# A two-layer decoder trunk on one core: memory normalised at evacuation, announced branches, the last expert pair by halves, the final norm applied at evacuation

## The reference

```python
def reference(...):
    mem_n = rms_norm(mem, norm_mem)
    for i in range(DEPTH):
        h = rms_norm(x, norm_mix[i])
        ...
            x = x + conformer_conv(h, ...)      # layer 0
        ...
            x = x + gla_mixer(h, ...)           # layer 1
        x = x + mem_cross_attn(rms_norm(x, norm_xattn[i]), mem_n, xa_w_q[i], xa_w_kv[i], xa_w_o[i])
        x = x + hier_moe(rms_norm(x, norm_ffn[i]), ...)
    return rms_norm(x, norm_final)

def rms_norm(x, g):
    y = xf * lax.rsqrt(jnp.mean(xf * xf, axis=-1, keepdims=True) + EPS)
    return (y * g.astype(jnp.float32)).astype(x.dtype)
```

## Time and profile before

| | us |
|---|---|
| median of three runs | 1923.87 |
| runs | 1920.25, 1923.87, 1925.53 |
| profiled execution | 1920.17 |
| its span in the profile | 1918.0 |
| PE busy | 1864.5 |
| DVE busy | 583.6 |
| ACT busy | 373.6 |
| POOL busy | 159.9 |

### The profile page before, as it was taken

One profiled execution on the slowest core, in us unless ns is written; L12 is line 12 of the kernel. 1 busy time (PEld: TensorE's weight loads), 2 busy tenths in 40 slices (PEclk: granted clock), 3 DMA queues, 4 the chain that ended last, 5 costly groups with the idle time before them and its releaser, 6 DMA issues.

```text
span 1918.0 us, 18457 instructions
## 1 busy us (share of the span) xinstructions
PE 1864.5 (97%) x7584; PEld 924.7 (48%) x7584; DVE 583.6 (30%) x1104; ACT 373.6 (19%) x629; POOL 159.9 (8%) x151
## 2 busy tenths in 40 slices
PE   6999999998999999999999999999989999999997
PEld 5445644545445454444344444454454444445443
DVE  3899221223122222222212322213222222222223
ACT  2333211212111011111124232122111111111113
POOL 0466210010000000000020000100100000000001
PEclk9999999998999999999999999999989999999998
DMA  9214422102999999999861211302169999999992
GB/s 352 74 46 169 174 88 88 74 17 105 414 404 406 412 403 416 405 412 406 336 224 44 88 44 44 132 1 91 44 260 415 404 413 407 413 406 403 415 411 88
DMA packets 89869, 477.08 MB, mean 249 GB/s; under 512 B 7662, under 2 KB 8092, under 8 KB 40236
## 3 DMA queue, kind: packets, MB, share of 16 engines
q1 hardware_dynamic: 88636, 470.90, 61.2%
q0 software_dynamic: 592, 2.63, 0.5%
q10 hardware_dynamic: 544, 2.22, 0.3%
HBM read 471.53 MB, written 4.19 MB: 248 GB/s over the span
## 4 chain that ended last, share of the span: by engine, by line
PE 90%; DVE 7%; ACT 1%; issue 1%; DMA 0%; SPq 0%; DVEq 0%; ACTq 0%
PE PS L617 23%; PE PS L435 17%; PE PS L391 13%; PE PS L632 12%; PE PS L655 7%; PE PS L672 7%; DVE PS L1752 5%; PE PS L920 3%; PE PS L530 2%; PE PS L442 1%; PE PS L662 1%; PE PS L644 1%; PE PS L681 1%; DVE PS L1750 1%; PE PS L875 0%
## 5 line engine op out<-in xcount | busy, mean ns | idle before, releaser
L435 PE MATMUL PS<-hT,ring 128*128 128x512 f32 x640 | 279.4, 596 | 4.1 <-ACT hT L1149 3.4
L632 PE MATMUL PS<-ring,hT 128*64 128x512 f32 x1024 | 226.8, 595 | 2.7 <-ACT hT L1250 2.7
L617 PE MATMUL PS<-ring,hT 128*64 128x512 f32 x1024 | 226.3, 595 | 1.3 <-DVE small L1631 1.3
L617 PE MATMUL PS<-ring,xg 128*64 128x512 f32 x1024 | 226.8, 595 | 0.0
L1640 DVE TENSOR_TENSOR xT<-PS,xT 128x512 f32<-128x512 f32 x256 | 158.5, 681 | 211.6 <-PE PS L655 211.6
L435 PEld LDWEIGHTS PS<-hT,ring 128*128 128x128 f32 x640 | 121.4, 191 | 153.3 <-issue 152.4
L617 PEld LDWEIGHTS PS<-ring,hT 128*64 128x64 f32 x1024 | 73.9, 137 | 132.9 <-issue 131.2
L617 PEld LDWEIGHTS PS<-ring,xg 128*64 128x64 f32 x1024 | 72.4, 137 | 132.4 <-issue 132.2
L632 PEld LDWEIGHTS PS<-ring,hT 128*64 128x64 f32 x1024 | 70.7, 137 | 135.1 <-issue 127.9
L1666 DVE TENSOR_TENSOR ylo<-PS,yhi 128x1024 fp32r<-128x1024 f32 x32 | 39.2, 1224 | 301.7 <-ACT yhi L1255 301.7
L655 PE MATMUL PS<-onehotT,yhi 128*128 128x512 f32 x256 | 115.0, 449 | 3.6 <-DVE ylo L1666 3.6
(11 more groups left out here) (263 smaller groups left out, 1768.8 us busy)
## 6 DMA issues: line engine op xcount, KB each, us to landing
ring<-in_moe_w_gate SPq DMA_DIRECT2D x128, 1024.0 KB, 11.2
ring<-in_moe_w_up SPq DMA_DIRECT2D x128, 1024.0 KB, 12.1
ring<-in_moe_w_down SPq DMA_DIRECT2D x128, 1024.0 KB, 9.0
ring<-in_xa_w_kv SPq DMA_DIRECT2D x16, 1024.0 KB, 7.3
ring<-in_gla_w_in SPq DMA_DIRECT2D x12, 1024.0 KB, 12.8
ring<-in_conv_w_in SPq DMA_DIRECT2D x8, 1024.0 KB, 14.2
ring<-in_xa_w_q SPq DMA_DIRECT2D x8, 1024.0 KB, 6.8
ring<-in_xa_w_o SPq DMA_DIRECT2D x8, 1024.0 KB, 6.9
```

The source lines that it names most:

```text
L435: mm = pe.matmul(bank(b), w[:, k * 512 + m * P:k * 512 + (m + 1) * P], src[:, k, :], start=(k == 0), stop=(k == C - 1))
L617: mm = pe.matmul(PS[e * SL:(e + 1) * SL, kind * BANK:(kind + 1) * BANK], x[:, k, (2 * (p % 2) + e) * SL:(2 * (p % 2) + e + 1) * SL], ring[ ...
L632: mm = pe.matmul(PS[e * SL:(e + 1) * SL, (2 + half) * BANK:(3 + half) * BANK], hidT[:, k, e * SL:(e + 1) * SL], ring[:, pair_slot(l, 4 + e ...
```

## The change

It has four parts. The memory is transposed as it was loaded, in two transfers with a semaphore each; its reciprocal norms are spread over the partitions by two products with diagonals (key `rbm`) and multiplied in, with the gain, when the transposes are evacuated; `mem_k(0, 0)` waits chunk by chunk. The three small loads ahead of the memory go to ACT's queue. In both layers the last pair's down projection is computed by output halves, with the transposed one-hot between them, and `yhi`, `ylo` and the scatter follow by halves. The branch over the overflow code is written out on PE, ACT and DVE and announced by a hint, placed behind pair 13 on PE and behind pair 8 on ACT and DVE; in layer 1 PE's waits for the last accumulates are moved behind the sums. At the end PE transposes `xT` itself; the gain `norm_final` is loaded as a row, broadcast to all partitions by a transfer of POOL's, and multiplied in at DVE's evacuations, or by POOL behind ACT's for the three blocks in `GAINED`; ACT loads its table first and only squares; POOL adds five squares and DVE the other three; the output is stored in eight half tiles.

```diff
 HOTS = NQ + TT - 1
...
 
...
         osum = small[:, 12:28]
...
                     for m in (2 * jj, 2 * jj + 1):
-                        mm = group(bank(b, (m % 2) * NMEM, (m % 2 + 1) * NMEM),
-                                   lambda k: w[:, k * 512 + m * P:k * 512 + (m + 1) * P],
-                                   lambda k: memT[:, k, :], C)
+                        for k in range(C):
+                            if l == 0 and i == 0 and m == 0:
+                                pe.wait_ge(mem_chunk, k + 1)
+                            mm = pe.matmul(bank(b, (m % 2) * NMEM, (m % 2 + 1) * NMEM),
+                                           w[:, k * 512 + m * P:k * 512 + (m + 1) * P], memT[:, k, :],
...
 
+                def down_half(p, half):
+                    pe.wait_ge(g["hidT_ready"], NP * r + p + 1)
+                    for k in range(FC):
+                        if k % 2 == 0:
+                            for e in range(2):
+                                loaded(p, 4 + e, k // 2)
+                        for e in range(2):
+                            mm = pe.matmul(PS[e * SL:(e + 1) * SL, (2 + half) * BANK:(3 + half) * BANK],
+                                           hidT[:, k, e * SL:(e + 1) * SL],
+                                           ring[:, pair_slot(l, 4 + e), k * D + half * 512:k * D + (half + 1) * 512],
+                                           start=(k == 0), stop=(k == FC - 1))
+                    mm.then_inc(g["y_full"], 1)
...
                         b, done = use(p, 1 + c)
                         for w in (yhi, ylo):
                             mm = pe.matmul(bank(b), w[:, c * P:(c + 1) * P], onehotT[:, :],
...
-                    down(p)
-                    if more:
-                        gather(q + 1, p, 10, 4 * s + 2)
-                    one_hot_T(p)
+                    if p < NP - 1:
+                        down(p)
+                        if more:
+                            gather(q + 1, p, 10, 4 * s + 2)
+                        one_hot_T(p)
+                    else:
+                        down_half(p, 0)
+                        one_hot_T(p)
+                        down_half(p, 1)
...
+                    if main and p == NP - 3:
+                        ahead = pe.mark_branch_hint_location()
...
-            pe.wait_ge(mem_ready, 2)
             for j in range(4):
-                transposes(("mt", j), [mem_tm[:, mt, c * P:(c + 1) * P] for c in (2 * j, 2 * j + 1) for mt in range(2)])
-            for j in range(4):
-                pe.wait_ge(*read(("mt", j)))
+                take(("mt", j))
+            for mt in range(2):
+                pe.wait_ge(s_mld[mt], 16)
+                for c in range(C):
+                    b = plan.at[("mt", c // 2)][0]
+                    mm = pe.transpose(bank(b, c % 2 * NMEM + mt * P, c % 2 * NMEM + (mt + 1) * P),
+                                      mem_tm[:, mt, c * P:(c + 1) * P], ident[:, :])
+                    if mt and c % 2:
+                        mm.then_inc(bank_full[b], 1)
+            b = take(("rbm",))
+            for mt in range(2):
+                pe.wait_ge(mem_ready, mt + 1)
+                mm = pe.matmul(bank(b, mt * P, (mt + 1) * P), ones[:, :], dg[:, mt, :], start=True, stop=True)
+            mm.then_inc(bank_full[b], 1)
             mem_k(0, 0)
...
-                worst = moe_segment(l, 0)
-                with pe.If(worst > SL):
+                worst, ahead = moe_segment(l, 0)
...
+                nc.switch_bb(f"pe_on{l}")
+                if l == 0:
+                    for b in range(3):
+                        pe.wait_ge(seg[l][f"x_read{b}"], PER_ROUND)
 
             moe(0)
...
-            for c in range(C):
-                wait_h(pe, LAST, c)
+            def turn_out(c, t):
+                if c % 4 == 0:
+                    take(("out", t, c // 4), (0, 1, 2, 3, 5, 6, 7, 4)[t + c])
+                b = plan.at[("out", t, c // 4)][0]
+                mm = pe.transpose(bank(b, c % 4 * P, (c % 4 + 1) * P), xT[:, c, t * P:(t + 1) * P], ident[:, :])
+                if c % 4 == 3:
+                    mm.then_inc(bank_full[b], 1)
+
+            for c in range(4):
+                wait_x(pe, LAST, c)
+                for t in range(TT):
+                    turn_out(c, t)
+            pe.wait_ge(norm_sum, LAST - 1)
+            token_sums(("rs", LAST), [dg[:, :, :].rearrange("p t s -> p (t s)")], 4)
+            for b in range(3):
+                pe.wait_ge(seg[1][f"x_read{b}"], PER_ROUND)
             for t in range(TT):
-                for half in range(2):
-                    if (t, half) == (2, 0):
-                        norm_sums(LAST)
-                    transposes(("out", t, half), [hT[:, 4 * half + j, t * P:(t + 1) * P] for j in range(4)])
...
-            vector_rows(sp, list(VROWS)[:NFIRST], s_vfirst)
-            sp.dma_start(mem_tm[:, :, :], a["mem"].rearrange("b (t p) d -> p (b t) d", p=P)).then_inc(s_mld, 16)
+            for i in range(2):
+                sp.dma_start(mem_tm[:, i, :], a["mem"].rearrange("b (t p) d -> p (b t) d", p=P)[:, i, :]
+                             ).then_inc(s_mld[i], 16)
...
-            for t in range(TT):
-                for half in range(2):
-                    sp.wait_ge(*read(("out", t, half)))
-                sp.dma_start(o_dram[t], x_tm[:, t, :]).then_inc(s_out, 16)
-            sp.wait_ge(s_out, 16 * TT)
+            for half in range(2):
+                cols = slice(half * 512, (half + 1) * 512)
+                for t in range(TT):
+                    if (t, half) in GAINED:
+                        sp.wait_ge(out_gained, GAINED.index((t, half)) + 1)
+                    else:
+                        sp.wait_ge(*read(("out", t, half)))
+                    sp.dma_start(o_dram[t][:, cols], x_tm[:, t, cols]).then_inc(s_out, 16)
...
-            norm_adds(LAST)
+            pool.dma_start(gain_row, a["norm_final"].rearrange("(o d) -> o d", o=1).to_broadcast([P, D])).then_inc(s_gain, 16)
+            for c in range(1, 5):
+                pool.wait_ge(sq_ready, C * (LAST - 2) + c + 1)
+                if c > 1:
+                    pool.wait_ge(early_adds, c - 1)
+                pool.tensor_tensor(rms, hT[:, c, :], hT[:, 0, :] if c == 1 else rms, ALU.add).then_inc(early_adds, 1)
+            pool.wait_ge(s_gain, 16)
+            for n, (t, half) in enumerate(GAINED):
+                cols = slice(half * 512, (half + 1) * 512)
+                pool.wait_ge(out_scaled, n + 1)
+                pool.tensor_tensor(x_tm[:, t, cols], x_tm[:, t, cols], gain_row[:, cols], ALU.mult).then_inc(out_gained, 1)
...
+                    else:
+                        act.activation(yhi[:, 0:512], bank(2), ACT.Copy).then_inc(g["yhi_done"], 1)
...
+                    if p == NP - 1:
+                        act.wait_ge(g["y_full"], YS * r + NP + 1)
+                        act.activation(yhi[:, 512:1024], bank(3), ACT.Copy).then_inc(g["yhi_done"], 1)
...
                               w[j * WDW_ROWS:(j + 1) * WDW_ROWS, :]).then_inc(s_wdw, 16)
             act.wait_ge(s_constp, NCONST)
...
-            act.wait_ge(s_mld, 16)
             ebf = EB[:, :, :].rearrange("p a t -> p (a t)")
             for mt in range(2):
+                act.wait_ge(s_mld[mt], 16)
                 link(act.activation(ebf, mem_tm[:, mt, :], ACT.Square, accum_out=mstat[:, mt:mt + 1]))
...
+            act.activation(small[:, 150:151], ones[:, 0:1], ACT.Sqrt)
             for c in range(C):
-                square(LAST, c)
-                gain(LAST, c)
+                wait_x(act, LAST, c)
+                act.activation(hT[:, c, :], xT[:, c, :], ACT.Square).then_inc(sq_ready, 1)
             norm_root(LAST)
             act.wait_ge(rb_ready, 2)
-            for t in range(TT):
-                evacuate(("out", t, 1), x_tm[:, t, 512:1024], scale=rrec[:, t:t + 1])
+            for t, half in GAINED:
+                evacuate(("out", t, half), x_tm[:, t, half * 512:(half + 1) * 512], scale=rrec[:, t:t + 1])
+                act.wait_ge(*read(("out", t, half)))
+                act.sem_inc(out_scaled, 1)
...
+                    dve.wait_ge(g["yhi_done"], YS * r + p + 1)
+                    n = 1024 if p < NP - 1 else 512
+                    dve.tensor_tensor(ylo[:, 0:n], PS[:, 2 * BANK:2 * BANK + n], yhi[:, 0:n].bitcast(F32),
                                       ALU.subtract).then_inc(g["ylo_done"], 1)
...
-                accumulate(NP, range(0, C))
+                        ahead = dve.mark_branch_hint_location()
+                accumulate(NP, range(0, 1))
+                dve.wait_ge(g["yhi_done"], YS * r + NP + 1)
+                dve.tensor_tensor(ylo[:, 512:1024], bank(3), yhi[:, 512:1024].bitcast(F32),
+                                  ALU.subtract).then_inc(g["ylo_done"], 1)
+                accumulate(NP, range(1, C))
...
-                worst = moe_segment(l, 0)
-                with dve.If(worst > SL):
+                worst, ahead = moe_segment(l, 0)
```

(35 more changed lines are left out.)

54 lines of the change are left out of this document (38 added, 16 removed).

## The result

| | us |
|---|---|
| before, median of four runs beside it | 1922.06 (1919.31 to 1925.53) |
| changed, median of four runs | 1904.49 (1904.17 to 1905.78) |
| ratio, 95% interval | 0.9909, 0.989 to 0.9928 |
| forecast | 1911.1, range 1904.0 to 1918.0 |
| profiled execution, before and changed | 1920.17 and 1904.18 |

The kernel is faster by 0.9%, as forecast, and by more than its sum: the profiled executions differ by 16.0 us, the sum had 12.75.

What follows compares the result with a forecast made beforehand. TensorE, busy 97% of the span, was taken as the bound. Gains 2.6 + 0.95 + 2.2 + 1.7 + 5.3 = 12.75 took 1920.17 to 1907.4, carried to the median as 1911.1 us; range 1904 to 1918.

Steps and rivals of the forecast that it cites:

- Start, 2.6: Program start: mem_k starts at 14.15, when its weights land, 4.6 sooner, less 2.0 at the low clock; gain 2.6 us.
- raised the clock before 18.76: Program start: PE's half-rate transposes had raised the clock before mem_k; without them mem_k starts at the low level, losing 2.0.
- Last pair by halves, layer 0, 0.95: End of layer 0's MoE: the scatter starts at 955.7 and the last accumulate ends at 962.2, not 963.15; gain 0.95 us.
- Branches, layer 0, 2.2 and clock 1.7: End of layer 0's MoE: announced branches let PE resume 2.2 us sooner; without the low clock behind it, 1.7 more.
- rival A: Branches of both layers: the announcement does nothing, layer 0 keeps its low clock, gains total 6.3, time 1917.6 us; chance 20%.
- Rival C: PE's MoE pairs: the announced block displaces the next, two crossings per layer at 3 us each, time 1929.6 us; chance 5%.
- well ahead of the branch: Sign at the end of layer 0's MoE: the instruction packet of 16 KB would come well before the branch.
- The banks rotate by one until the first attention; no row prices that, I leave 0.5 either way: PSUM banks from the start to the first attention: rotation shifts by one, left unpriced at 0.5 us either way.
- End, 5.3: Program end after layer 1: reworked final norm and output end at 1912.7 against 1918.0; gain 5.3 us, bounds 4.3 to 6.4.
- ACT loads its table at once: Program end: ACT loads its table (1.28 us) right when yhi's second half is ready at 1891.7, and squares from 1893.3.
- The sum: Whole kernel: gains of start, halves, branches, clock and end add to 12.75 us, taking the profiled 1920.17 to 1907.4.
- The step to the median: Whole kernel: the profiled execution lay 3.7 us below the three-run median 1923.87, so 1907.4 was carried to 1911.1.

Runs made afterwards that it cites:

- e7: The changed kernel with the last pair's down projection, yhi and ylo in one piece again: 1905.12 us, ratio 0.9920 to the kernel before.
- e1: The changed kernel with its rebuilt branches but no announcement on any engine: 1911.58 us, ratio 0.9943 to the kernel before.
- e6: The changed kernel with the announcement on PE alone, none on ACT and DVE: 1906.87 us, ratio 0.9925 to the kernel before.
- e12: The kernel before with only the rebuilt branches announced on PE, ACT and DVE: 1918.20 us, ratio 0.9989 to the kernel before.
- e3: The changed kernel with the PSUM bank rotation put back to that of the kernel before: 1906.88 us, ratio 0.9919 to the kernel before.

## Why the forecast was right, and where it was not

The direction was right, and so were the branches and the halves of layer 0. The range held by only 0.5 us, and 2.85 of the 16.0 us came from a term that the forecast put at nothing.

- **Start, 2.6: measured 4.0 in this pair.** The bound was named rightly (the weights), their landing was put 1.1 too late (14.15 against 13.06), and the stretch at the lower level cost 1.7, not 2.0. The chain ahead of it came out near (12.4 forecast, 11.9 measured) by luck: the memory landed at 6.19 and not at 8.35, but the transposes had not left the chain, for the diagonals, ready at 8.28, waited until 9.89 for PE, which ran its 16 transposes at half rate until 10.09. And no row shows that work on PE "raised the clock before 18.76": the granted clock reads 1.00 over those slow transposes too (13.8 to 17.5 before, 6.4 to 10 after). Single pairs say little here: the transposes of x start at 30.3 to 32.7 in the three profiles with the old start and at 28.4 to 31.5 in the nine with the new one. Their means are 31.8 and 29.3, so 2.6 fits better than 4.0.
- **Last pair by halves, layer 0, 0.95: measured 1.12**, and by e7 2.1, of which 1.0 is its low-clock stretch.
- **Branches, layer 0, 2.2 and clock 1.7: measured 2.14 and 1.70.** e1, e6 and e12 take rival A down. The sequential prefetch of the Trainium skill ("Runtime: NRT & Kernel Launch", "Instruction fetch mechanics") fits the branches that aren't announced (3.24 in e1), not PE's and most of DVE's that are. Rival C's block crossings show nowhere. Two signs did not come as written: DVE's wait is 0.79, not below 0.5, and no packet of code "well ahead of the branch" sets the changed kernel apart. On the queue q8 a packet starts at 957.5 as PE's scatter ends, and in e1 too, at 958.9; what is gone is the second one, which e1 has at 962.5. When the announced code was loaded isn't shown.
- **"The banks rotate by one until the first attention; no row prices that, I leave 0.5 either way"** is the step that failed. The rotation reaches the last attention, and a row did price it: the 2.03 us wait stood in the trace of before, at a bank taken by name. In the profiled pair it is worth 2.2 and a low-clock stretch of 1.7, less the 1.0 lost again, 2.85 net.
- **End, 5.3: measured 4.0.** "ACT loads its table at once" is the mis-sized term. Moved by 11.6 to the changed kernel's time, the forecast has the first square at 1881.7, POOL from 1883.0, the sum closed at 1889.2; measured are 1883.47, 1884.69 and 1891.51. 1.8 of the 2.3 is ACT's wait at the branch, the rest POOL slowed by DVE from 1.39 to 1.53. PE's sums then ran at the lower level, 0.9 longer, and 1.6 came back behind POOL's last product (3.0 forecast as 4.6; the 4.86 that the forecast starts from is 4.89 by its rows).
- **The sum** had 12.75; the parts measured give 4.0 - 0.2 + 4.95 + 2.85 + 4.0 = 15.6 (the 0.2 is a low-clock stretch in layer 0 that both have).
- **The step to the median** was off by 3.4. The profiled execution of before lay 3.7 below the median of the three runs, and I carried that over; the changed kernel's lies 0.3 below its own. Together with the sum's 3.2 (16.0 - 12.75) this makes the 6.6 between 1911.1 and 1904.49.

**Open:** why ACT's code seems to have been fetched at its branch in layer 1 with the announcement, early or late, as without it, and not in e7, and why that cost at most 0.78 in layer 0; why DVE's announcement failed in layer 0 of e12 alone; and what the start gives by itself.

## What to carry to other kernels

Look at every buffer or PSUM bank that is taken by name inside a rotation: who had it last is decided by every `take` ahead of it, and one more or fewer, far away, makes or removes a wait. Announce a branch on the engine that the chain runs through, and then look in the trace, engine by engine, whether the "issue" wait behind it is gone. Price an idle stretch of TensorE of some microseconds together with the slow matmuls that can follow it: here they cost up to nearly as much again, though not behind each such stretch (e3).
